# The last layer normalisation of a decoder layer, with shift and beta as an outer product on TensorE

## What is computed

```python
def layer_norm(x, g, b):
    mu = mean(x); var = mean((x - mu)**2)
    return (x - mu) * rsqrt(var + LN_EPS) * g + b

ffn = (silu(h @ w_ffn_gate) * (h @ w_ffn_up)) @ w_ffn_down      # w_ffn_down: 5632 x 2048
h = layer_norm(DEEPNORM_ALPHA * h + ffn, ln2_g, ln2_b)          # over the 2048 features of a token
```

## Time and profile before

| | us |
|---|---|
| median of 3 runs | 1413.8 (1413.75 to 1414.63) |
| the profiled execution, own time | 1415.67 |
| its span, first to last instruction | 1413.9 |
| TensorE busy in the span | 1383.2 (98%) |
| VectorE busy | 890.6 (63%) |
| ScalarE busy | 655.2 (46%) |
| GpSimd busy | 61.8 (4%) |

### The profile page before, as it was taken

How to read it: one execution, slowest core, us unless ns; L and a number is a source line. 1 busy time by engine, 2 the same in 40 slices (tenths; PEclk the granted TensorE clock), 3 DMA queues, 4 the chain that set the end, 5 groups by cost and what they waited for, 6 DMA issues and landing times.

```text
span 1413.9 us, 24366 instructions
## 1 busy us (share of the span) xinstructions
PE 1383.2 (98%) x8784; PEld 1247.4 (88%) x8784; DVE 890.6 (63%) x1294; ACT 655.2 (46%) x920; POOL 61.8 (4%) x31
## 2 busy tenths in 40 slices
PE   7999999999999999998999999999999999999996
PEld 7999999999999999886888888888888888888884
DVE  5677756777567676557766666666666664445445
ACT  5456546465364644335544444444444443334332
POOL 1000211202111000000000000000000000000002
PEclk9999999999999999999999999999999999999998
DMA  7646444444444677554556555555555565556562
GB/s 267 197 148 177 152 135 134 134 148 134 134 147 145 211 224 236 196 167 146 183 183 199 184 194 185 193 191 182 192 191 187 189 248 193 182 190 190 168 206 89
DMA packets 80414, 252.70 MB, mean 179 GB/s; under 512 B 17664, under 2 KB 17920, under 8 KB 80256
## 3 DMA queue, kind: packets, MB, share of 16 engines
q1 hardware_dynamic: 80384, 252.31, 54.7%
HBM read 248.08 MB, written 2.10 MB: 177 GB/s over the span
## 4 chain that ended last, share of the span: by engine, by line
PE 94%; DVE 3%; SPq 1%; DMA 1%; ACT 1%; issue 0%; ACTq 0%; DVEq 0%
PE ps L829 22%; PE ps L832 12%; PE ps L818 10%; PE ps L819 9%; PE ps L820 9%; PE ps L841 8%; PE ps L842 8%; PE ps L840 8%; PE ps L946 1%; PE ps L936 1%; PE ps L972 1%; PE ps L973 1%; DVE wlo L418 1%; SPq L298 1%; DMA xrow<-x 1%; PE ps L958 1%
## 5 line engine op out<-in xcount | busy, mean ns | idle before, releaser
L418 DVE TENSOR_TENSOR wlo<-raw,whi 128x1024 fp32r<-128x1024 f32 x438 | 532.3, 1223 | 305.5 <-ACT whi L462 304.8
L462 ACT ACTIVATE whi<-raw 128x1024 fp32r<-128x1024 f32 x454 | 478.8, 1057 | 498.5 <-PE ps L842 191.4
L829 PE MATMUL ps<-hT,whi 128*128 128x512 f32 x1408 | 489.6, 391 | 2.6 <-DVE tmp L1662 1.5
L832 PE MATMUL ps<-hT,wlo 128*128 128x256 f32 x1408 | 397.0, 282 | 0.0
L829 PEld LDWEIGHTS ps<-hT,whi 128*128 128x128 f32 x1408 | 264.2, 188 | 60.3 <-DVE hT L1644 3.1
L832 PEld LDWEIGHTS ps<-hT,wlo 128*128 128x128 f32 x1408 | 266.1, 189 | 0.0
L818 PE MATMUL ps<-xT,whi 128*128 128x256 f32 x784 | 225.2, 287 | 2.9 <-ACT zT L481 2.6
L819 PE MATMUL ps<-xT,whi 128*128 128x256 f32 x784 | 219.7, 280 | 0.0
L820 PE MATMUL ps<-xT,wlo 128*128 128x256 f32 x784 | 219.6, 280 | 0.0
L818 PEld LDWEIGHTS ps<-xT,whi 128*128 128x128 f32 x784 | 148.3, 189 | 3.9 <-issue 3.2
L819 PEld LDWEIGHTS ps<-xT,whi 128*128 128x128 f32 x784 | 148.3, 189 | 0.4
(11 more groups left out here) (238 smaller groups left out, 1531.5 us busy)
## 6 DMA issues: line engine op xcount, KB each, us to landing
raw<-slabs SPq DMA_DIRECT2D x454, 512.0 KB, 3.4
xrow<-x SPq DMA_DIRECT2D x4, 512.0 KB, 6.4
rows<-x SPq DMA_DIRECT2D x4, 512.0 KB, 5.9
gb<-ln_rows SPq DMA_DIRECT2D x4, 512.0 KB, 7.2
gb<-ln_rows SPq DMA_DIRECT2D x1, 2048.0 KB, 8.0
u<-ustage SPq DMA_DIRECT2D x16, 64.0 KB, 3.5
yb<-u SPq DMA_DIRECT2D x16, 48.0 KB, 3.1
out<-rows SPq DMA_DIRECT2D x3, 256.0 KB, 2.5
```

The source lines that it names most:

```text
L418: unit.tensor_tensor(wlo[:, s, :], raw[:, s, :], whi[:, s, :].bitcast(F32), ALU.subtract).then_inc(done, 1 + empty_after)
L462: nc.scalar.activation(whi[:, s, :], raw[:, s, :], ACT.Copy).then_inc(hi_ready, 1 + empty)
L829: mm(ps[:, bank, :], hi, src[:, kt].rearrange("p a t -> p (a t)"), start=(first and n == 0), stop=False)
L832: ins = mm(ps[:, bank, TOK:512], lo, src[:, kt, 0, :], start=False, stop=done)
```

## The change

Gamma, beta and the shift s = -mean * rstd are brought together by out = (rows * gamma) * rstd + (s * gamma + beta).

- **Rows of gamma and beta for TensorE.** In the first down panel ScalarE copies gamma and beta into `lnrow` (four copies of 64x1024, rounded high parts) and VectorE replaces half of the partitions by the low parts (four subtractions of 32x1024), so that partitions 0 to 31, 32 to 63, 64 to 95 and 96 to 127 hold gamma high, gamma low, beta high and beta low. VectorE also clears `scol` and writes two columns of ones.
- **Gamma early.** VectorE multiplies finished chunks by gamma (`times_gain`, 512 columns each) during the next panel: both tiles of panels 1 and 2 and tile 1 of panel 0, five instructions; a sixth, for tile 1 of the last panel, stands at the end.
- **The last panel.** It is written out apart. Token tile 1 goes to two banks of 256 columns (banks 1 and 6), so its 132 matmuls of 512 columns become 264 of 256. In the last four slabs the order is tile 0, then the first half of tile 1 (`split_done`), then the second. Ahead of the last slab's six matmuls TensorE transposes tile 0's `scol`.
- **VectorE at the end.** For each tile: statistics, `rstd`, `sm`, `scol` (the high and low part of s in columns, L1815 and L1816 of the kernel after) and `rdiag`, a diagonal matrix of rstd. It normalises two chunks of 512 of tile 0 by two instructions each and three chunks of tile 1 by one instruction each, which adds rows * rstd to the s * gamma + beta in PSUM.
- **TensorE at the end.** `turn_shift` transposes `scol`, ScalarE copies the result to `srow`, and `offset` multiplies it with `lnrow`: one matmul of 512 columns for a chunk. For chunks 1 and 2 of tile 0 and chunk 0 of tile 1 a float32 matmul with `rdiag` adds rows * rstd in the same bank, and ScalarE copies the finished bank to `rows` (`out_copy`).
- **GpSimd** has nothing at the end any more. SP issues eight stores of 512 columns, 256 KB each.

The diff, cut to its core:

```diff
+            sy.wait_ge(out_ready, 1)
+            store(0, 0, 512)
+            for n in (1, 2):
+                sy.wait_ge(out_act, n)
+                store(0, n * 512, n * 512 + 512)
+            sy.wait_ge(out_ready, 2)
+            store(0, 1536, D)
+            for n in (1, 2):
+                sy.wait_ge(out_ready, 2 + n)
+                store(1, n * 512, n * 512 + 512)
+            sy.wait_ge(out_act, 3)
+            store(1, 0, 512)
+            sy.wait_ge(out_ready, 5)
+            store(1, 1536, D)
+            sy.wait_ge(out_stored, 8 * 16)
...
-            po.wait_ge(in_gb, 80)
-            for t in range(2):
-                c2 = OUT_CUT[t][2]
-                po.wait_ge(out_normed, t + 1)
-                nc.gpsimd.tensor_tensor(rows[:, t, c2:], rows[:, t, c2:], gb[:, 0, c2:], ALU.mult).then_inc(out_scaled, 1)
-                po.wait_ge(out_scaled, t + 1)
-                nc.gpsimd.tensor_tensor(rows[:, t, c2:], rows[:, t, c2:], gb[:, 1, c2:], ALU.add).then_inc(out_ready_pool, 1)
...
+            ac.wait_ge(in_gb, 80)
+            for k in range(4):
+                high(0, DOWN0, 4, k + RING)
+                half, cut = slice(64 * (k // 2), 64 * (k // 2) + 64), slice(1024 * (k % 2), 1024 * (k % 2) + 1024)
+                ac.wait_ge(slab_used, DOWN0)
+                nc.scalar.activation(lnrow[half, cut], gb[half, k // 2, cut], ACT.Copy).then_inc(lnrow_hi, 1)
+            with ac.Fori(1, DOWN_PER - 1) as i:
...
+            def s_copy(t, bank):
+                ac.wait_ge(s_psum, t + 1)
+                nc.scalar.activation(srow[:, t, :], ps[:, bank, 0:P], ACT.Copy).then_inc(s_copied, 1)
+            def out_copy(t, n, bank, count):
+                ac.wait_ge(x_psum, count)
+                nc.scalar.activation(rows[:, t, n * 512:n * 512 + 512], ps[:, bank, :], ACT.Copy).then_inc(out_act, 1)
+            norm_root(0, 3)
+            s_copy(0, 7)
+            norm_root(1, 4)
+            out_copy(0, 1, 2, 1)
+            out_copy(0, 2, 3, 2)
+            s_copy(1, 0)
+            out_copy(1, 0, 4, 6)
...
-            with pe.Fori(0, 2) as i:
+            with pe.Fori(0, 1) as i:
...
+            def last_part(k, t):
+                def part(bank, c0, c1):
+                    return row_tile(bank, (v + k) % RING, t, act, (2 * k, 2 * k + 1), k == 0, k == DOWN_PER - 1, c0, c1)
+                if t == 0:
+                    part(0, 0, 512)
+                else:
+                    part(1, 0, 256)
+                    part(6, 256, 512).then_inc(slab_used, 1)
+            for k in range(DOWN_PER - RING):
+                late_low(v + k)
+                for t in range(2):
+                    if k == 0:
+                        row_bank(m + t)
+                    last_part(k, t)
+            for k in range(DOWN_PER - RING, DOWN_PER):
+                late_low(v + k)
+                ins = row_tile(0, (v + k) % RING, 0, act, (2 * k, 2 * k + 1), False, k == DOWN_PER - 1)
+            ins.then_inc(half_done, 1)
+            for k in range(DOWN_PER - RING, DOWN_PER):
+                ins = row_tile(1, (v + k) % RING, 1, act, (2 * k, 2 * k + 1), False, k == DOWN_PER - 1, 0, 256)
+            ins.then_inc(split_done, 1)
+            def turn_shift(t, bank):
+                pe.wait_ge(s_ready, t + 1)
+                nc.tensor.transpose(ps[:, bank, 0:P], scol[:, t, :].bitcast(F32), ident).then_inc(s_psum, 1)
+            for k in range(DOWN_PER - RING, DOWN_PER):
+                row_tile(6, (v + k) % RING, 1, act, (2 * k, 2 * k + 1), False, k == DOWN_PER - 1, 256, 512).then_inc(slab_used, 1)
+                if k == DOWN_PER - 2:
+                    turn_shift(0, 7)
+            def offset(t, n, bank, scaled):
+                pe.wait_ge(s_copied, t + 1)
+                cut = slice(n * 512, n * 512 + 512)
+                ins = mm(ps[:, bank, :], srow[:, t, :], lnrow[:, cut], start=True, stop=not scaled)
+                if scaled:
+                    pe.wait_ge(diag_ready, t + 1)
+                    ins = mm(ps[:, bank, :], rdiag[:, t, :], rows[:, t, cut], start=False, stop=True)
+                ins.then_inc(x_psum, 1)
+            pe.wait_ge(lnrow_lo, 4)
+            offset(0, 1, 2, True)
+            offset(0, 2, 3, True)
+            pe.wait_ge(row_free, 2 + 8 + 2 * FT + 7)
+            turn_shift(1, 0)
+            offset(1, 1, 5, False)
+            offset(1, 2, 7, False)
+            offset(1, 3, 0, False)
+            offset(1, 0, 4, True)
...
+            def times_gain(n, t):
+                st.wait()
+                r_ = rows[:, t, n * 512:n * 512 + 512]
+                st(V.tensor_tensor(r_, r_, gb[:, 0, n * 512:n * 512 + 512], ALU.mult))
+            def lnrow_low(k):
+                half, cut = slice(64 * (k // 2) + 32, 64 * (k // 2) + 64), slice(1024 * (k % 2), 1024 * (k % 2) + 1024)
+                ve.wait_ge(lnrow_hi, k + 1)
+                V.tensor_tensor(lnrow[half, cut], gb[half, k // 2, cut], lnrow[half, cut].bitcast(F32), ALU.subtract
+                                ).then_inc(lnrow_lo, 1)
...
+                    if n == 0 and k in (10, 12, 14, 16):
+                        lnrow_low(k // 2 - 5)
+                    if n == 0 and k == 18:
+                        st(V.memset(scol[:].bitcast(F32), 0.0)); st.wait()
+                        st(V.memset(scol[:, :, 64:P:32].bitcast(F32), 1.0))
...
-                down_residual(3, t)
-                statistics(t)
-                inverse_root(t, 3 + t)
-                if t == 0:
-                    ve.wait_ge(in_gb, 80)
-                V.scalar_tensor_tensor(sm[:, t:t + 1], moments[:, t, 0:1], -1.0, rstd[:, t:t + 1], ALU.mult, ALU.mult
-                                       ).then_inc(shift_ready, 1)
-                for c0, c1 in zip(OUT_CUT[t], OUT_CUT[t][1:]):
-                    r_ = rows[:, t, c0:c1]
-                    st(V.scalar_tensor_tensor(r_, r_, moments[:, t, 0:1], gb[:, 0, c0:c1], ALU.subtract, ALU.mult)); st.wait()
-                    V.scalar_tensor_tensor(r_, r_, rstd[:, t:t + 1], gb[:, 1, c0:c1], ALU.mult, ALU.add).then_inc(out_ready, 1)
...
+            def shift(t):
+                st(V.scalar_tensor_tensor(sm[:, t:t + 1], moments[:, t, 0:1], -1.0, rstd[:, t:t + 1], ALU.mult, ALU.mult)); st.wait()
+                st(V.tensor_copy(scol[:, t, 0:64:32], sm[:, t:t + 1].to_broadcast([P, 2]))); st.wait()
+                V.tensor_tensor(scol[:, t, 1:2], sm[:, t:t + 1], scol[:, t, 0:1].bitcast(F32), ALU.subtract).then_inc(s_ready, 1)
+                V.tensor_scalar(rdiag[:, t, :], ident, rstd[:, t:t + 1], None, ALU.mult).then_inc(diag_ready, 1)
+            def centred(t, n):
+                r_ = rows[:, t, n * 512:n * 512 + 512]
+                st(V.scalar_tensor_tensor(r_, r_, moments[:, t, 0:1], gb[:, 0, n * 512:n * 512 + 512], ALU.subtract, ALU.mult))
+            def scaled(t, n):
+                st.wait()
+                r_ = rows[:, t, n * 512:n * 512 + 512]
+                V.scalar_tensor_tensor(r_, r_, rstd[:, t:t + 1], gb[:, 1, n * 512:n * 512 + 512], ALU.mult, ALU.add).then_inc(out_ready, 1)
+            def half_residual(e):
+                if e == 0:
+                    ve.wait_ge(split_done, 1)
+                else:
+                    ve.wait_ge(slab_used, DOWN0 + 4 * DOWN_PER)
+                r_ = rows[:, 1, 1536 + 256 * e:1792 + 256 * e]
+                st(V.scalar_tensor_tensor(r_, r_, ALPHA, ps[:, (1, 6)[e], 0:TOK], ALU.mult, ALU.add)); st.wait()
+                st(V.bn_stats(stats[:, 1, 3 + e, :], r_))
+            down_residual(3, 0)
+            statistics(0)
+            inverse_root(0, 3)
+            shift(0)
+            centred(0, 0)
+            scaled(0, 0)
+            half_residual(0)
+            half_residual(1)
+            statistics(1, 5)
+            centred(0, 3)
+            inverse_root(1, 4)
+            shift(1)
+            scaled(0, 3)
+            times_gain(3, 1)
+            st.wait()
+            for n, bank, count in ((1, 5, 3), (2, 7, 4), (3, 0, 5)):
+                r_ = rows[:, 1, n * 512:n * 512 + 512]
+                ve.wait_ge(x_psum, count)
+                V.scalar_tensor_tensor(r_, r_, rstd[:, 1:2], ps[:, bank, :], ALU.mult, ALU.add).then_inc(out_ready, 1)
```

More of the change, by code:

```diff
@@ L193, in build @@
         assert o <= a3 + FT * 2 * TOK * 4 and a3 + FT * 2 * TOK * 4 + 4 * PAIRS <= nc.sbuf_usable_end
+        lnrow = at("lnrow", a1, [P, D], F32R)
+        scol = at("scol", a2, [P, 2, P], F32R)
+        srow = at("srow", a2 + 1024, [P, 2, P], F32R)
+        rdiag = at("rdiag", a2 + 2048, [P, 2, P])
         bpar = at("bpar", a1, [P, 2, PAIRS, GROUP])
@@ L242, in build @@
             "ffn_silu", "ffn_prod", "act_hi", "act_lo", "out_ready"))
-        shift_ready, out_normed, out_scaled, out_ready_pool = (sem(n) for n in (
-            "shift_ready", "out_normed", "out_scaled", "out_ready_pool"))
+        lnrow_hi, lnrow_lo, split_done, s_ready, s_psum, s_copied, diag_ready, x_psum, out_act = (sem(n) for n in (
```

(28 more changed lines are left out.)

21 lines of the change are left out of this document (5 added, 16 removed).

## The result

| | us |
|---|---|
| before, median of 4 runs | 1414.2 (1413.75 to 1414.86) |
| changed, median of 4 runs | 1425.0 (1424.25 to 1425.88) |
| ratio | 1.0077, 95% interval 1.0063 to 1.009 |
| changed, profiled execution, own time | 1425.28 |
| its span | 1423.5 |

The forecast was 1410.3 with a range up to 1412.2. The time lies outside, and it has moved the other way.

What follows compares the result with a forecast made beforehand. TensorE carries 94% of the chain of waits, so only the 13.04 us tail could shrink: VectorE's steps, then queued stores, end the span near 1410.4 instead of 1413.9; 3.5 off 1413.8 gives 1410.3 us, range 1409.4 to 1412.2.

Steps and rivals of the forecast that it cites:

- the second sentence's conclusion: Whole kernel: TensorE's columns stay the same, so only the 13.04 us behind its last down matmul can be shortened.
- TensorE's last down matmul as far from the start as before, within 0.3: End of the down panels: a sign that the forecast is right; TensorE's down work was to end at 1400.97, before 1400.86.
- rival B: Last panel: the split's extra 132 matmuls cost 0.09 us each, TensorE ends 11.9 us later, time 1422; chance 0.03.
- the rest 0.04 for a stall in the panels: Panels before the tail: chance 0.04 left over for a stall there, with no size given.
- The split: Last down panel: tile 1's 132 matmuls become 264 of half width, the pairs costing nothing; 0.233 and 0.117 us each.
- VectorE's tail: After TensorE's last down matmul: VectorE's last instruction 6.2 to 6.5 us later, against 10.08 before.
- TensorE and ScalarE: Tail: the fourth offset with its float32 matmul ends at 1406.4, ScalarE's copy at 1407.0, 0.3 before VectorE's last.
- rival A: Tail: TensorE's clock falls to 1.2 GHz from 1404.4 on, gain only 2.4 us, time 1411.4; chance 0.14.
- The argument against A from the stage of transposes: Stage from 653.97: only transposes with gaps, nothing from 659 to 660, yet the clock stayed at 1.00.
- The stores: End: four stores issued in 1.5 us queue, 256 KB taking 0.68 us each; last data at 1409.4, span end 1410.45.
- The sum without the shift: Whole kernel: span from 1413.9 to 1410.4, 3.5 us less, taken off the median 1413.8.
- The cause that was seen, GpSimd beside VectorE: Tail of the kernel before: about 3.7 us lost in long VectorE instructions, put down to GpSimd, which the change removes.

Runs made afterwards that it cites:

- experiment 1: Changed kernel with the statistics tile moved to a free part of the kmat area, large tiles back at their old addresses: 1412.6 us, ratio 0.9985.
- experiment 2: Kernel before with 64 unused bytes behind the statistics tile, so the large tiles stand where the changed kernel has them: 1428.1 us, ratio 1.0095.
- experiment 14: Experiment 1's kernel with the last panel not split, tile 1 in one bank by matmuls of 512 columns: 1413.1 us, ratio 0.9985.

## Why the prediction was wrong

**The step that failed** is the second sentence's conclusion: "The change leaves TensorE's columns alone, so what can be won lies behind its last matmul." Columns and waits were right, the price of a column was not. I took every matmul up to the last panel over from the trace of before, and the first line of the diff moved their operands by 64 bytes. It cost 12.2 us by the ends of TensorE's down work in the changed kernel and in experiment 1 (1413.55 and 1401.38), 12.4 by their times, and 13.3 in the kernel before (experiment 2). The sign "TensorE's last down matmul as far from the start as before, within 0.3" caught it. The range had no case for it: besides rival B, "the rest 0.04 for a stall in the panels" was the only place for a slower TensorE.

**Rival B** gave 1422 and looks like a hit by its number. That is luck: the price was set on the 132 extra matmuls of the last panel, 0.09 each, and the split cost 119.2 x 264 - 233.2 x 132 ns = 0.7 us in experiment 1, not 11.9.

**The split, "cost nothing"**: 0.7 by the paces, and TensorE ended 0.5 later than before instead of 0.11. The rows for 256 columns were those of another tile pair, and the pace differs from pair to pair. By experiment 14 the split is neither gain nor loss where the clock stays, 0.7 on TensorE against 0.8 on VectorE; by the one trace in which the clock fell without it, the end behind VectorE's last sum is 4.7 us instead of 3.9.

**VectorE's tail** was forecast at 6.3 from the last down matmul and measured at 6.06 (6.07 in experiment 1). The terms held: statistics of 256 columns 0.43 (0.45), small steps 0.20 apart, L1821 0.68, the sums 0.69 each. Three small instructions a tile are new (L1815 to L1817), as this sum had it; the text on the change says four.

**TensorE and ScalarE** ended at 1406.4 and 1407.0 in the forecast, 5.4 and 6.0 behind the last down matmul; in the changed kernel 5.4 and 6.0.

**The clock** stayed at 1.00 until the end, as forecast against rival A; experiment 14 shows how near the other case was. The argument against A from the stage of transposes was weaker than it looked: the clock stayed at 1.00 behind that stage in the trace of before, and was 0.50 there in those of experiments 2 and 14, with the same gaps.

**The stores** are the term that was too small. Behind VectorE's last sum the forecast had 3.2 us, measured 3.9. It queued four stores at 384 KB/us from the earlier trace rows; data moved from 1419.2 to beyond 1422.4, 1024 KB in 3.3 us, so about 310 KB/us. That takes 0.6 of the 3.5.

**The sum without the shift**: forecast -3.5; experiment 1 -2.6 in the span, -2.2 in the time. The missing 0.9 of the span are 0.7 behind VectorE's last sum (0.6 of it the stores' rate) and 0.4 of TensorE's end (the split), less 0.2 that VectorE's tail was shorter than forecast. The cause that was seen, GpSimd beside VectorE, was right: two such instructions cost 4.2 when put back.

## What to carry to other kernels

Before costing an edit, list which tiles it moves: one tile that grows in front of others in a hand-made layout moves all behind it, and here 64 bytes cost over five times what the edit gained (12.4 against 2.2 us). When stages that were not edited change, compare matmuls per 100 us at an equal clock, and pad the old kernel by the same bytes: one run tells a layout effect from the edit. GpSimd instructions beside VectorE's with two operands in SBUF are worth taking out of a tail: here they cost 4.2 us.
